# A two-block mixer kernel: first attention on split fp32r operands, modulation on TensorE in the recurrent stage, and values multiplied ahead of the turns

## Chip, cores and metric

The kernel runs on one core of a Trainium2 chip. The metric is the device time of one execution in microseconds, the median of the runs shown. TensorE is PE in the rows, its weight loads PEld, VectorE is DVE, ScalarE ACT, GpSimd POOL, and SP is the queue of SyncE, which issues most DMAs.

## What is computed

Two transformer blocks run one after the other on 512 tokens of width 1024, all in fp32. Each has a mixer and a mixture of experts. The change lies in the first mixer, in the modulation vectors of both blocks, and in the order of one shared loop:

```python
# modulation: one row per condition, six parts of 1024 columns
mod = silu(c) @ w_ada + b_ada                    # block 1
mod_2 = silu(c_2) @ w_mod_2 + b_mod_2            # block 2; parts 0 and 1 for c_ctx_2 too

# first mixer: u = layer_norm(x) * (1 + sc) + sh; proj = u @ w_in, split in q, k, v, f, xb, gb
cum = cumsum(log_sigmoid(f + b_f))               # 8 heads x 512 tokens
for i in range(4):                               # 128 queries each, keys up to their own tile
    logits = q_i @ k[:kend].T / 8 + cum_q - cum_k[:kend], causal mask
    out_i = softmax(logits) @ v[:kend]
# recurrent branch: conv over xb, gates r and ig by 64x64 blocks, h = a h + u, times gelu(gb)
mixed = concat(rms_norm(attn), rms_norm(lru)) @ w_out
```

The second block's mixer has two attentions of its own, a neighbourhood one with a bias and a grouped one, both of 8 heads and 4 query tiles, over 512 or 640 and over 768 keys.

## The kernel before

**Stages.** The program is a list of stages (`stage`, L64): each allocates its semaphores, gives every engine one instruction stream, and ends with a barrier of all engines (L70). So no engine goes on before the last one has run out, a queue of DMA issues included. In order: `setup`, `modulation` "mod1", `normalise` and `turn`, `project` "in1", `gates_and_lru`, `attention` "at1", `norm_branches` "nb1", `out_projection`, `normalise`, then the experts, then block two.

**Precision.** Products that need fp32 are made in two ways. `split3` (L45) takes operands split in a high and a low fp32r half and makes three products (L47 to L49); ACT rounds the high half and DVE subtracts to get the low one. Plain fp32 matmuls need no split; each shows in the trace as two instructions.

**Modulation.** Class `Modulation` (L285) makes one part of 1024 columns per job as a sum over 1024 rows of the weights: a quarter of a job, 256 rows or 1 MB, is loaded to a slot, and DVE adds it in two steps of 128 rows, each scaled by one silu column (L331, L335). Then TensorE sums the accumulator over the partitions by 8 products with a column of ones (`sum`, L353), DVE adds the bias (`put`, L365 to L371), and where a row is wanted in DRAM too, POOL stores it after all loads, element by element (`store`, L379), and waits for it to land. The steps are dealt out to turns of the stage beside which the jobs run, `per` of them to each (rounded up). Four jobs of block 1 run beside the ten chunks of "in1" (DVE makes the low half of chunk n+3 first, then its turn's steps; two slots, loaded from POOL's queue), eight jobs of block 2 beside the 32 units of "at1" (six slots, loaded from SP's queue).

**Input projection.** `project` (L548) streams ten chunks of w_in: SP loads, ACT makes the high half, DVE the low one, TensorE multiplies, ACT empties PSUM. TensorE takes the column sums of finished jobs two chunks later, and those of the last two chunks' turns at its end.

**Recurrent stage.** `gates_and_lru` (L690). POOL zeroes tiles (L711 to L713). SP loads the forget-gate weights (L718) and bias (L720), waits for the zeroing, loads 16 blocks of gate weights (L726), and then issues 64 small DRAM-to-DRAM copies of relative-position rows for block two (L732); nobody waits for those before block two. DVE runs the convolution (L743, L746) with the split of the forget weights in it (L753, L755), then the long chain of elementwise steps of both branches: softplus as a series (`log1p_series`), the cumulative sum `cum` (L780), the gates, the scan (L798) and the last product (L800). TensorE multiplies the forget logits (8 columns of weights, `split3`), then eight gate matmuls in plain fp32 (L814) into eight PSUM banks; ACT applies the sigmoids (L827).

**First attention.** `attention` (L842), 32 units of a head and a query tile. Per unit TensorE makes the scores in plain fp32 (L878: q by k with K = 64, minus `cum` by a selector with K = 8, the mask by the identity), DVE takes the maximum (L926), ACT the exponential (L962), DVE the inverse (L932) and the scaling (L935), TensorE turns the probabilities (L888), ACT copies them out of PSUM (L972), TensorE multiplies by the values (L898), DVE copies the result (L939). DVE's modulation steps lie between.

**Later attentions.** `attend` (L982) is the pipeline of block two. Same unit, but with operands split in fp32r halves: scores (L1051), turns (`fill`, L1037), ACT rounds the turned probabilities (L1095), DVE makes their low half (L1136), value products for two tiles at a time in two halves of a pair (`mix`, L1074 to L1076), ACT and DVE split the result (L1130, L1185). A turn waits for DVE's scaling (L1159) and for its PSUM bank; the first half of a pair waits for the low half of the pair's last tile (TensorE's loop, L1081):

```python
for u in range(STEPS):
    if u < NU:
        score(u)
    if 2 <= u <= NU + 1:
        turn_probs(u - 2)
    if mixing(u) is not None:
        mix(*mixing(u))
```

DVE's step u is: maximum of u (L1147), inverse and scaling of u-1, low half of u-2, then splits that hooks ask for.

## Time and profile before

| | |
|---|---|
| median of 3 runs | 3230.81 us (3228.14 to 3244.43) |
| profiled execution | 3230.41 us, of which the span 3228.7 us |
| mean granted TensorE clock over the span | 0.876 |
| busy, share of the span | PE 81%, PEld 66%, DVE 71%, ACT 48%, POOL 10% |
| HBM | 692.68 MB read, 227 GB/s over the span |
| "in1" | 69.5 to 199.5 us |
| recurrent stage | 199.5 to 267.7 us |
| first attention | 267.7 to 464.2 us |
| neighbourhood and grouped attention | 1394.4 to 1513.4 and 1513.4 to 1632.3 us |

### The profile page before, as it was taken

How to read it: one execution, taken by the hardware profiler on the slowest of the kernel's cores; microseconds unless marked ns; L12 is line 12 of the kernel's file. 1: busy time of each engine (PE TensorE's matmuls, PEld its weight loads, DVE VectorE, ACT ScalarE, POOL GpSimd, SP SyncE). 2: the span in 40 equal slices, each digit the busy share in tenths (PEclk: the TensorE clock that was granted, in tenths of full speed). 3: DMA queues.
4: the chain of work that ended last, by engine and by line, in shares of the span. 5: the costliest groups of instructions: out<-in, count | busy, mean ns of one | idle time of the engine just before them, and what ended most of it. 6: DMA issues, size and time to landing. Idle time of an engine off the chain costs nothing. (4 is left out here: it accounts for less than half of the span.)

```text
span 3228.7 us, 37865 instructions
## 1 busy us (share of the span) xinstructions
PE 2611.3 (81%) x12822; PEld 2126.6 (66%) x12822; DVE 2276.4 (71%) x2213; ACT 1539.0 (48%) x1420; POOL 316.6 (10%) x260
## 2 busy tenths in 40 slices
PE   2966975389996299857886379999999999999991
PEld 2844645367774199746766358778778778778771
DVE  5566645378885611277843579999999999999985
ACT  2212121066673323244622057666777666777660
POOL 0100000013331000000000011111111111111110
PEclk9985557589998599878998579999999999999995
DMA  5724421189995223100021189999999999999994
GB/s 203 240 46 149 123 73 52 61 328 379 377 371 217 95 67 110 57 1 27 1 86 59 40 293 362 363 370 367 367 366 362 364 368 369 367 366 362 364 343 150
DMA packets 256873, 731.66 MB, mean 227 GB/s; under 512 B 29779, under 2 KB 69906, under 8 KB 256594
## 3 DMA queue, kind: packets, MB, share of 16 engines
q1 hardware_dynamic: 232306, 653.93, 55.9%
q0 software_dynamic: 19872, 72.39, 5.8%
q10 hardware_dynamic: 4608, 4.20, 0.4%
q8 instruction: 52, 0.85, 0.1%
q14 instruction: 35, 0.29, 0.0%
HBM read 692.68 MB, written 39.37 MB: 227 GB/s over the span
## 5 line engine op out<-in xcount | busy, mean ns | idle before, releaser
L48 PE MATMUL psum_all<-sb_ring_r,sb_arena_r 128*128 128x512 f32 (+1 forms) x2912 | 1072.5, 368 | 1.2 <-issue 1.2
L152 DVE TENSOR_TENSOR sb_ring_r<-sb_ring,sb_hi_ring 128x2048 fp32r<-128x2048 f32 x297 | 674.4, 2287 | 277.3 <-ACT sb_hi_ring L143 271.6
L47 PE MATMUL psum_all<-sb_hi_ring,sb_arena_r 128*128 128x512 f32 (+1 forms) x1880 | 665.9, 354 | 51.6 <-DVE sb_ring_r L152 47.2
L49 PE MATMUL psum_all<-sb_hi_ring,sb_arena_r 128*128 128x512 f32 (+1 forms) x1880 | 660.0, 351 | 0.2 <-issue 0.2
L48 PEld LDWEIGHTS psum_all<-sb_ring_r,sb_arena_r 128*128 128x128 f32 x2912 | 558.0, 192 | 91.3
L143 ACT ACTIVATE sb_hi_ring<-sb_ring 128x2048 fp32r<-128x2048 f32 x297 | 563.4, 1913 | 103.0 <-DMA sb_ring<-in_w_gu_dram 30.6
L152 DVE TENSOR_TENSOR sb_ring_r<-sb_ring,sb_arena_r 128x2048 fp32r<-128x2048 f32 x258 | 581.4, 2283 | 23.5 <-ACT sb_arena_r L143 23.2
L143 ACT ACTIVATE sb_arena_r<-sb_ring 128x2048 fp32r<-128x2048 f32 x258 | 485.5, 1915 | 194.2 <-DMA sb_ring<-in_w_gu_dram 188.9
L47 PEld LDWEIGHTS psum_all<-sb_hi_ring,sb_arena_r 128*128 128x128 f32 x1880 | 360.4, 192 | 108.9 <-DVE sb_ring_r L152 49.4
L47 PE MATMUL psum_all<-sb_arena_r 128*128 128x512 f32 x1032 | 415.3, 402 | 12.6 <-DVE sb_ring_r L152 7.9
L49 PE MATMUL psum_all<-sb_arena_r 128*128 128x512 f32 x1032 | 412.0, 399 | 0.0
L49 PEld LDWEIGHTS psum_all<-sb_hi_ring,sb_arena_r 128*128 128x128 f32 x1880 | 359.5, 191 | 52.7 <-issue 1.3
L47 PEld LDWEIGHTS psum_all<-sb_arena_r 128*128 128x128 f32 x1032 | 195.3, 189 | 71.3 <-DVE sb_ring_r L152 28.9
L49 PEld LDWEIGHTS psum_all<-sb_arena_r 128*128 128x128 f32 x1032 | 196.1, 190 | 42.8
L1691 POOL DMA_INDIRECT y_dram<-sb_arena x52 | 95.1, 1829 | 997.8 <-ACT sb_arena L1842 988.9
L511 PE MATMUL psum_all<-sb_ident,sb_arena 128*128 128x128 f32 x176 | 40.2, 383 | 171.3 <-PEq L70 164.6
L511 PEld LDWEIGHTS psum_all<-sb_ident,sb_arena 128*128 128x128 f32 x176 | 27.7, 193 | 183.6 <-issue 166.2
L1677 POOL COPY sb_arena<-sb_ids 128x1 int32 (+1 forms) x54 | 24.5, 454 | 982.5 <-POOLq L70 467.4
L1817 ACT ACTIVATE sb_arena_r<-psum_all 128x1024 fp32r<-128x1024 f32 x54 | 55.1, 1020 | 115.0 <-PE psum_all L1720 96.8
L1892 DVE TENSOR_TENSOR sb_arena_r<-psum_all,sb_arena_r 128x1024 fp32r<-128x1024 f32 x54 | 65.6, 1215 | 62.0 <-ACT sb_arena_r L1817 62.0
L1837 ACT ACTIVATE sb_arena_r<-psum_all 128x1024 fp32r<-128x1024 f32 (+1 forms) x52 | 45.7, 878 | 116.6 <-PE psum_all L1729 116.6
L47 PE MATMUL psum_all<-sb_arena_r,sb_hi_ring 128*128 128x512 f32 (+1 forms) x224 | 86.9, 388 | 14.9 <-DVE sb_ring_r L152 14.9
(359 smaller groups left out, 3287.4 us busy)
## 6 DMA issues: line engine op xcount, KB each, us to landing
sb_ring<-in_w_gu_dram SPq DMA_DIRECT2D x272, 1024.0 KB, 7.1
sb_ring<-in_w_dn_dram SPq DMA_DIRECT2D x136, 1024.0 KB, 9.3
sb_ring<-in_w_e_gate_dram SPq DMA_DIRECT2D x36, 1024.0 KB, 7.3
sb_ring<-in_w_e_up_dram SPq DMA_DIRECT2D x36, 1024.0 KB
sb_ring<-in_w_e_down_dram SPq DMA_DIRECT2D x36, 1024.0 KB, 7.7
sb_ring<-in_w_in_dram SPq DMA_DIRECT2D x27, 1024.0 KB, 5.5
sb_ring<-in_w_mod_dram SPq DMA_DIRECT2D x24, 1024.0 KB, 5.8
sb_arena<-in_w_ada_dram POOLq DMA_DIRECT2D x16, 1024.0 KB, 5.6
```

The lines of the kernel that those rows point to most:

```text
L47: eng.matmul(out, a[0], b[0], start=start, stop=False)
L48: eng.matmul(out, a[0], b[1], start=False, stop=False)
L49: return eng.matmul(out, a[1], b[0], start=False, stop=stop)
L143: act.activation(s.hi[c % len(s.hi)], s.raw[c % SLOTS], ACT.Copy).then_inc(s.hi_made, 1)
L152: dve.tensor_tensor(s.lo[c % SLOTS], s.raw[c % SLOTS], s.hi[c % len(s.hi)].bitcast(F32), ALU.subtract).then_inc(s.lo_made, 1)
L511: ins = pe.transpose(k.psum[:, i % 2, t * P:(t + 1) * P], src[:, t, i * P:(i + 1) * P], k.ident[:])
L1677: pool.tensor_copy(idx, R.ids[:, bass.ds(j, 1)]).then_inc(s.idx, 1)
L1691: pool.indirect_dma_start(m.y, bass.IndirectOffsetOnAxis(ap=to_row.bitcast(U32), axis=0), ysb.rearrange("p h n -> p (h n)"), None).then_in ...
L1817: act.activation(part, banks, ACT.Copy).then_inc(s.x_hi, 1)
L1837: act.activation(part, banks, ACT.Copy).then_inc(s.h_hi, 1)
L1892: dve.tensor_tensor(part, banks, turned_banks(x_hi[p], KD)[0].bitcast(F32), ALU.subtract).then_inc(s.x_lo, 1)
```

## The change

The change moves the modulation, replaces the attention and swaps two calls.

- **Modulation.** Of the eight jobs that ran beside the attention two (parts 4 and 5 of block 2) now run beside "in1", which has six jobs. The other parts (0 to 3; 0 and 1 for both conditions) are multiplied on TensorE in the recurrent stage: 16 chunks of 1 MB (two groups of 2048 columns, 8 row blocks), four fp32 products of 512 columns each with a stationary operand of two silu columns, in PSUM banks 4 to 7. The gate matmuls share banks 0 to 3 and wait for ACT from the fifth on. Bias, gain and the stores follow in the next stage on POOL and SP; a turn in `norm_branches` brings the parts to columns.
- **Recurrent stage.** The forget logits are made three times, at rows 0, 32 and 64, so that `cum` can be split in three fp32r parts. SP's order: forget weights, zeroing, three bias loads, gate weights, the 16 chunks, then the 64 copies.
- **First attention.** `attention` is gone; `forgetting_attention` builds products for `attend`: scores of K = 128 on zero-padded fp32r halves, with `cum` by one fp32r product and the mask by another. The result isn't split.
- **`attend`**, for all three: TensorE multiplies the values ahead of the turns.

```diff
@@ gates_and_lru
+            pool.memset(w_parts.bitcast(F32), 0.0)
+            pool.memset(k.small[:, 100:101], 0.0)
             pool.memset(w_r, 0.0)
             pool.memset(w_i, 0.0).then_inc(s.zeroed, 1)
...
-            sp.dma_start(b_f, a["b_f"].rearrange("o h -> h o")).then_inc(s.f_loaded, 16)
             sp.wait_ge(s.zeroed, 1)
+            for group in range(3):
+                sp.dma_start(b_f[32 * group:32 * group + NH], a["b_f"].rearrange("o h -> h o")).then_inc(s.f_loaded, 16)
...
+            def load_mod(n):
+                c, kd = mod_chunks[n]
+                if n >= MOD_SLOTS:
+                    sp.wait_ge(s.mod_used, n - MOD_SLOTS + 1)
+                sp.dma_start(k.ring[:, n % MOD_SLOTS, :], a["w_mod_2"][0, kd * P:(kd + 1) * P, c * CHUNK:(c + 1) * CHUNK]
+                             ).then_inc(mod_landed[n % MOD_SLOTS], 16)
...
+            for n in range(len(mod_chunks)):
+                load_mod(n)
             rows = k.rpb_rows.rearrange("(r i) (h g c) -> h r i g c", i=16, h=NH, c=48)
...
-            dve.tensor_tensor_scan(cum, t1, z, 0.0, ALU.mult, ALU.add)
+            dve.tensor_tensor_scan(cum, t1, z, 0.0, ALU.mult, ALU.add).then_inc(s.summed, 1)
+            dve.wait_ge(s.part_hi, 1)
+            dve.tensor_tensor(t1, cum, fixed.parts[0:NF].bitcast(F32), ALU.subtract).then_inc(s.part_rest, 1)
...
+            def modulate(n):
+                c, kd = mod_chunks[n]
+                pe.wait_ge(mod_landed[n % MOD_SLOTS], 16 * (n // MOD_SLOTS + 1))
+                for b in range(CHUNK // 512):
+                    ins = pe.matmul(k.psum[32 * c:32 * c + 2, 4 + b, :], k.silu[:, KD + kd:KD + kd + KD + 1:KD],
+                                    k.ring[:, n % MOD_SLOTS, 512 * b:512 * b + 512], start=kd == 0, stop=kd == KD - 1)
+                ins.then_inc(s.mod_used, 1)
...
             ins.then_inc(s.multiplied, 1)
+            for n in range(4):
+                modulate(n)
             pe.wait_ge(s.loaded, 16 * 4 * NJ)
...
+                if i >= 4:
+                    pe.wait_ge(s.gated, i - 3)
+                pe.matmul(k.psum[:, i % 4, :], w[:, j, :], xc[:, j, :], start=True, stop=True).then_inc(s.gates, 1)
+            for n in range(4, len(mod_chunks)):
+                modulate(n)
...
+            act.wait_ge(s.mod_used, len(mod_chunks))
+            for c in range(2):
+                act.activation(mod_rows[32 * c:32 * c + 2], k.psum[32 * c:32 * c + 2, 4:8, :].rearrange("p b n -> p (b n)"),
+                               ACT.Copy).then_inc(s.mod_put, 1)
@@ attend
-                        pe.wait_ge(s.out_lo, h - 1)
+                        pe.wait_ge(s.out_hi, h - 1)
+                        if spec.splits:
+                            pe.wait_ge(s.out_lo, h - 1)
...
+                if mixing(u) is not None:
+                    mix(*mixing(u))
                 if 2 <= u <= NU + 1:
                     turn_probs(u - 2)
-                if mixing(u) is not None:
-                    mix(*mixing(u))
@@ forgetting_attention (new), products and values of one head
+        return [(cols, fixed.neg[:, h, :], fixed.parts[:, 0:n], True, False), (cols, q_hi, key_hi, False, False),
+                (cols, q_lo, key_hi, False, False), (cols, q_hi, key_lo, False, False),
+                (last, fixed.ident, fixed.causal, False, True)]
...
+        return [(v_hi[:, b, cols], v_lo[:, b, cols], b, int(b > 2 * pair), 2) for b in range(2 * pair + 2)]
...
+        def dve_step(dve, u, main):
+            if u < 2:
+                value_lo(dve, u)
+            if u % 8 == 4 and u < 24:
+                key_lo(dve, u // 8 + 1)
+            if u % TT == 1 and u < 28:
+                q_lo(dve, u // TT + 1)
@@ forgetting_attention, SP and POOL
+            sp.dma_start(bias_rows[0:2], b_mod[0:CHUNK].partition_broadcast(2)).then_inc(s.rows_loaded, 16)
...
+            sp.dma_start(k.mod_columns, mod_rows[0:2]).then_inc(s.rows_stored, 16)
...
+            pool.tensor_tensor(mod_rows[0:2], mod_rows[0:2], bias_rows[0:2], ALU.add).then_inc(s.row, 1)
@@ norm_branches
+            sp.dma_start(rows, columns[1]).then_inc(s.columns, 16)
...
+            pe.transpose(k.psum[:, 2, 0:4 * KD], rows, k.ident[0:4 * KD, 0:4 * KD]).then_inc(s.turned, 1)
@@ block_one_mixer
-             (w_1, 0, 5, 0, "plus one", mod["gt2"], None, gate[1:2, :])],
-             [(w_2, 1, 0, 1, "plain", mod["sh1_2"], None, None),
...
+             (w_1, 0, 5, 0, "plus one", mod["gt2"], None, gate[1:2, :]),
              (w_2, 1, 4, 1, "gain", mod["sc2_2"], g_ffn, gate[7:8, :]),
              (w_2, 1, 5, 1, "plain", mod["gt2_2"], None, gate[3:4, :])]]
```

In `setup` the selector `neg_sel` grows from 8 to 128 rows, by three selects in place of one (L243).

## Rows read from the trace of the kernel before

**Rows 1.** Five stages: us, busy of PE, PEld, DVE, ACT, POOL, clock, DMA, GB/s.

```profile
69.50:199.50 130.00, 123.04 (x640) 104.68 (x640) 61.66 (x46) 30.88 (x34) 15.25 (x20) 0.96 0.58 194
199.50:267.70 68.20, 16.12 (x40) 5.92 (x40) 56.59 (x81) 20.97 (x26) 1.03 (x3) 0.66 0.21 28
267.70:464.20 196.50, 185.64 (x560) 114.46 (x560) 115.50 (x203) 33.49 (x98) 3.53 (x4) 0.53 0.39 129
...
1394.40:1513.40 119.00, 89.21 (x624) 82.18 (x624) 98.31 (x199) 63.50 (x136) 1.89 (x2) 0.87 0.00 1
1513.40:1632.30 118.90, 95.69 (x652) 84.26 (x652) 96.03 (x182) 70.27 (x150) 0.00 (x0) 0.93 0.06 19
```

**Rows 2.** Groups by line, first attention: busy, mean ns | idle before.

```profile
L335 DVE SCALAR_TENSOR_TENSOR sb_arena<-sb_ring,sb_silu,sb_arena 128x1024 f32<-128x1024 f32 x56 | 70.5, 1279 | 1.7
...
L926 DVE TENSOR_REDUCE sb_small<-psum_all 128x1 f32<-128x128 f32 (+3 forms) x32 | 15.7, 490 | 36.8 <-PE psum_all L878 36.6
...
L935 DVE TENSOR_SCALAR sb_arena<-sb_arena,sb_small 128x128 f32<-128x128 f32 (+3 forms) x32 | 12.4, 387 | 1.2
...
L932 DVE RECIPROCAL sb_small<-sb_small 128x1 f32<-128x1 f32 x32 | 4.9, 154 | 0.6 <-DVE sb_arena L335 0.2
```

**Rows 3.** Timeline, input projection's end: start us, us, engine, line.

```profile
164.88 0.71 POOL L317 DMA_DIRECT2D sb_arena<-in_w_ada_dram  x1 [7.13 <-DVEq L339]
...
170.30 2.67 DVE L335 SCALAR_TENSOR_TENSOR sb_arena<-sb_arena,sb_silu 128x1024 f32<-128x1024 f32 x2 [2.88 <-DMA sb_arena<-in_w_ada_dram]
...
198.37 0.38 ACT L1311 ACTIVATE sb_arena<-psum_all 128x256 f32<-128x256 f32 x1 [2.45 <-PE psum_all L49]
```

**Rows 4.** Timeline at the end of the first attention.

```profile
449.50 3.57 PE L353 MATMUL psum_all<-sb_ones,sb_arena 128*128 128x1 f32 x16
...
464.17 0.99 SPq L122 DMA_DIRECT2D sb_ring<-in_w_out_dram  x2
```

**Rows 5.** Timeline of the recurrent stage.

```profile
200.06 0.52 POOL L713 MEMSET sb_rows<- 128x512 f32 x1
200.61 5.85 SPq L726 DMA_DIRECT2D sb_rows<-in_w_rg_dram  x8
...
211.91 41.11 SPq L732 DMA_DIRECT2D rpb_rows<-rpb_pad  x64
```

**Rows 6.** Timeline, the first attention's first weights.

```profile
267.69 3.37 SPq L317 DMA_DIRECT2D sb_ring<-in_w_mod_dram  x6
...
273.05 1.41 DVE L331 TENSOR_SCALAR sb_arena<-sb_ring,sb_silu 128x1024 f32<-128x1024 f32 x2 [2.78 <-DMA sb_ring<-in_w_mod_dram]
```

**Rows 7.** Weight loads of the gate matmuls at full clock.

```profile
218.08 0.19 PEld L814 LDWEIGHTS psum_all<-sb_arena,sb_rows 128*128 128x128 f32 x1 [0.24 <-issue]
218.51 0.19 PEld L814 LDWEIGHTS psum_all<-sb_arena,sb_rows 128*128 128x128 f32 x1 [0.24 <-issue]
```

**Rows 8.** The same table, short windows: eight-column products, gates, gates, attention.

```profile
206.90:210.40 3.50, 3.47 (x15) 1.19 (x13) 3.46 (x6) 0.00 (x0) 0.00 (x0) 0.98 0.11 23
213.30:217.00 3.70, 3.70 (x5) 1.58 (x6) 3.05 (x20) 2.23 (x3) 0.00 (x0) 0.57 0.27 38
217.00:220.70 3.70, 3.70 (x10) 1.60 (x9) 3.56 (x6) 2.59 (x5) 0.00 (x0) 0.97 0.24 37
272.00:292.00 20.00, 20.00 (x50) 10.38 (x49) 17.67 (x29) 4.51 (x14) 0.00 (x0) 0.50 0.92 369
```

**Rows 9.** A group by form, neighbourhood attention.

```profile
L1136 DVE TENSOR_TENSOR sb_hi_ring<-psum_all,sb_hi_ring 128x512 fp32r<-128x512 f32 x32 | 21.9, 685 | 2.9 <-ACT sb_hi_ring L1095 2.8
```

**Rows 10.** Timeline of a step of the grouped attention.

```profile
1561.30 0.85 PE L1037 MATMUL psum_all<-sb_ident,sb_rows 128*128 128x128 f32 x6
...
1562.02 0.87 ACT L1095 ACTIVATE sb_hi_ring<-psum_all 128x512 fp32r<-128x512 f32 x2 [1.02 <-PE psum_all L1037]
...
1562.99 1.02 DVE L1136 TENSOR_TENSOR sb_hi_ring<-psum_all,sb_hi_ring 128x512 fp32r<-128x512 f32 x2
...
1563.05 0.86 PE L1051 MATMUL psum_all<-sb_arena_r 128*128 128x512 f32 x4
```

More of the change, by code:

```diff
@@ L1022, in attend, with _ @@
         load_ahead(nc, k, block, name, ahead)
+        if hooks.sync is not None:
+            @block.sync
+            def _(sp):
+                hooks.sync(sp)
         def bank(m, n):
@@ L1180, in _ @@
                 hooks.dve_step(dve, u, s)
-                if leaving(u - 1) is not None:
+                if spec.splits and leaving(u - 1) is not None:
                     h = leaving(u - 1)
@@ L1185, in _, with norm_branches @@
                     dve.tensor_tensor(out_lo, k.psum[rows, 6 + h % 2, :], out_hi.bitcast(F32), ALU.subtract).then_inc(s.out_lo, 1)
-def norm_branches(nc, k, name, branches, squares, ahead=()):
+def norm_branches(nc, k, name, branches, squares, ahead=(), columns=None):
     NJ = DA // P
     with stage(nc) as ctx:
-        s = sems(nc, ctx, name, "squared", "summed", "chain", "mean", "root", "whole", "hi")
+        s = sems(nc, ctx, name, "squared", "summed", "chain", "mean", "root", "whole", "hi", "columns", "loaded", "turned")
+        rows = k.rows[0:4 * KD, 0, 0:P]
         block = ctx.enter_context(nc.Block())
-        load_ahead(nc, k, block, name, ahead)
+        @block.sync
+        def _(sp):
+            sp.dma_start(rows, columns[1]).then_inc(s.columns, 16)
+            for i, src in enumerate(ahead):
+                sp.dma_start(k.ring[:, i, :].rearrange("p (a b) -> p a b", a=src.shape[1]), src).then_inc(s.loaded, 16)
+            sp.wait_ge(s.loaded, 16 * len(ahead))
         @block.vector
@@ L1235, in _ @@
                                ACT.Copy).then_inc(s.hi, 1)
-def split_tiles(nc, k, name, tiles, ahead=()):
-    with stage(nc) as ctx:
-        s = sems(nc, ctx, name, "hi")
-        flat = lambda t: t.rearrange("p j n -> p (j n)")
-        block = ctx.enter_context(nc.Block())
-        load_ahead(nc, k, block, name, ahead)
-        @block.scalar
-        def _(act):
-            for whole, hi, _ in tiles:
-                act.activation(flat(hi), flat(whole), ACT.Copy).then_inc(s.hi, 1)
-        @block.vector
-        def _(dve):
-            for i, (whole, hi, lo) in enumerate(tiles):
-                dve.wait_ge(s.hi, i + 1)
-                dve.tensor_tensor(flat(lo), flat(whole), flat(hi).bitcast(F32), ALU.subtract)
+            act.wait_ge(s.turned, 1)
@@ L1346, in block_one_mixer @@
                   [area(4096, 4, T), area(6144, 4, T)],
-                  ahead=[column_chunk(a["w_out"][0], 256 * h) for h in range(AHEAD)])
+                  ahead=[column_chunk(a["w_out"][0], 256 * h) for h in range(AHEAD)],
+                  columns=(k.mod_turned, k.mod_columns.rearrange("c (j p) -> (c j) p", p=P)))
     out_projection(nc, k, "out1", a["w_out"][0], mixed, k.gate_rows[0:1, :], k.arena[:, 0:D])
@@ L2394, in grouped_attention @@
     spec.n = lambda t: KEYS
+    spec.splits = True
     spec.bias = None
```

317 lines of the change are left out of this document (153 added, 164 removed).

## The prediction

> **What bounds the kernel now.** I read the page first, then a table of the stages the diff touches, then their timelines, and the engines' groups last. The page's slices show the expert stages holding TensorE and DMA at nine tenths; nothing of the diff is there. In the stage table [rows 1] the first mixer's attention takes 196.5 us: TensorE is busy for 185.6 of it at a mean clock share of 0.53, so it works at the lower of its two levels (1.2 GHz). DVE is busy for 115.5, of which 71 are modulation sums [rows 2]. The recurrent stage before it takes 68.2 and has TensorE idle for 52; the input projection before that is TensorE's (123 of 130). The two later attentions take 119.0 and 118.9 with DVE busy for 98.3 and 96.0. Stages are closed by a barrier, so each is a sum of its own. The profiled execution took 3230.4, the median is 3230.8: the sum goes against 3230.4.
>
> **Part 1: input projection, two more modulation jobs.** Jobs go from 4 to 6, steps from 32 to 48, and so from 4 to 5 per chunk. A quarter of a job needs two DVE steps (2.67, 2.9 with what lies between) and comes into one of two slots: POOL issues at 164.88 and DVE begins at 170.30, so 5.4 to land [rows 3]. Two slots give one quarter per (5.4 + 2.9)/2 = 4.15. I placed the 48 steps turn by turn, five behind each low half: the last quarter is done at about 200.5. TensorE used to end just before 198.4 [rows 3]; a fifth job's column sum stands in its way, 3.57 at the low clock [rows 4], 1.9 at the full one, which makes it 200.2. So both end together, the sixth sum (1.9) comes behind, and behind it something new: its row is stored to DRAM as 1024 single elements. In the old attention the same tail ran from the sum's end at 453.07 to the next stage's first issue at 464.17: 11.1 [rows 4]. The next stage starts at 200.5 + 1.9 + 11.1 = 213.5 where it started at 199.5: **+14** (12, if the sums are full speed and nothing lags; 19, if the quarters lag by one landing).
>
> **Part 2: recurrent stage.** Its DVE chain moves by 4 to 6 us (memsets, three bias loads, six split instructions ahead; three part copies and two subtractions behind) and ends near +74: no longer the end. Two queues are.
> TensorE: POOL clears 1152 more columns, 1.2 by the 512 columns in 0.52 [rows 5], and SP's three bias loads now stand behind that, 1.4; the gate-weight loads took from 200.61 to 211.91, 11.3 [rows 5]. So the first 1 MB of modulation weights is issued at +15.1 and used 5.4 later, as in the old attention (267.69 to 273.05) [rows 6]: +20.5. Each chunk is four products of plain fp32 over 512 columns. The gate matmuls are such products: two instructions each, 0.43 apart at full clock [rows 7], so 0.86 a product and 3.43 a chunk. That the stationary side has 2 columns buys nothing: the forget logits with 8 columns stream like others. DMA delivers at 369 GB/s [rows 8], 2.8 us per MB, ahead of 3.43. After the wait the clock is low for 3.7 us as in 213.3 to 217.0 (0.57), then 0.97 [rows 8]: 1.9 lost. Four chunks end at +36.1, the gates at +43.0, the next eight at +70.4, the last four at +84; two PSUM reads of 2048 columns end near +88.
> SP: load 16 waits for chunk 12 of TensorE, +70.4. Behind it, on the same queue, stand the 64 relative-position copies, which ran under the DVE chain before: 41.1 in a row, 0.64 each, back to back [rows 5]. They end at +111.9. With 0.8 to the next stage (as 198.75 to 199.5) 112.7 against 68.2: **+44.5**. So moving the sums to TensorE is not what costs; what costs is the copies that are now queued behind its loads.
> What no row shows is how two stationary columns of fp32 hold the clock. Bounds: the full level (+44.5), as fp32 products of 128 columns had it and as products with 8 stationary columns had it (0.98) [rows 8]; or the low one throughout, as the old attention, with products of K = 8 and 64 in fp32, had it while TensorE never paused [rows 1]. Low costs (12 x 3.43 + 6.9 - 1.9) = 46 more. I take the full level, as K is 128 here and the rows are back to back.
> The Trainium skill (TensorE: Matmul & The Clock Gate, "Why this matters for your kernels") holds that a TensorE kept busy without a break has the full clock; by that there is only the first bound, but the old attention contradicts it: busy, and low.
>
> **Part 3: first attention.** The modulation sums (71 us of DVE and their first products) leave. What DVE now does: maxima 15.7, inverses 4.9, scaling 12.4 [rows 2]; the low halves of turned probabilities, new here, have the maxima's sizes and speed (0.685 at 512 columns) [rows 9]: 15.7, as the maxima; splits of queries, keys and values, 8 + 4 of 512 columns and 2 of 1024: 10.7. Together 59.4. The first later attention has the same pipeline and took 119.0 for 98.3 of DVE [rows 1]: as a factor (1.21) that gives 72, as an addition (20.7) 80. Part of either is waits that I count below, so I take 74. ACT, 63.5 there, is beside it here too. TensorE per head: 20 score products, 10 turns, 18 value products. Six turns take 0.60 and nine value products 1.15 [rows 10], so 0.12 apiece, and the wide scores 0.16 and 0.22: 6.3 a head, 50 in all. POOL's four row operations and SP's small loads and stores end within some 30 us and are hidden by the rest; no 9 us store is left at the end.
> The new order adds a wait. At an even step the value products need the low half of step u-3, DVE's last act of step u-1; the turns now queue behind them, and behind the turns ACT's rounding and DVE's next low half. Value products 0.54 + turns and their reading 0.54 + rounding 0.42 against maximum, inverse and scale 0.94: 0.6 late. Every other even step has a query split ahead that covers it, so 8 times: 4.5. **Stage 78 against 196.5: -118.5.** Bounds: 69 (half of the 20.7 and no wait), and 105 at the low clock: 48 instructions at 0.23 and 1.2 for the wide ones make 11.8 a head, 95, and 10 of filling.
>
> **Part 4: the two later attentions** change only in that order. In the grouped one DVE has no idle time in a normal step; turns start at 1561.30, ACT reads at 1562.02 (first copy done 1562.62) and DVE takes it at 1562.99 [rows 10]: 0.37 to spare. The new order puts 1.15 of value products (T to the next scores at 1563.05, less 0.60) ahead and starts them with DVE's last low half: about 1.0 late, on 8 even steps (the other 8 follow a late query fill that gives the time back): +8. In the neighbourhood one 0.45 x 8: +4. **+12**; from -3 (TensorE fills its wait for the scale, and scores come earlier) to +24 (all 16 even steps).
> Setup (two more POOL selects, 2 us, under the loads), the branch norm (one small load ahead of w_out, a turn and a copy at the end of idle engines): 0.
>
> **Sum.** 14 + 44.5 - 118.5 + 12 = -48: 3230.4 - 48 = 3182, at the median's level too.
>
> **Rivals.**
> R1, the clock stays low in both new places. For it: 0.53 over the old attention with TensorE always busy; the row says that work alone does not raise it. Against it: 0.97 on fp32 gates, 0.87 and 0.93 in the later attentions, which have the same fp32r operands and the same turns. Recurrent stage +46, attention +27: 3255, slower. Low clock in the recurrent stage alone already eats the gain, and anything above 48 us on top turns the sign.
> The Trainium skill (same page, "Part 4: PE-mode transpose") says that transposes do not engage the full clock; by that the attention with its 80 turns might stay low. The grouped attention with six per step has 0.93, so the trace disagrees.
> R2, low clock for the modulation products alone: 3228, no change.
> R3, attention low alone: 3209.
> R4, the order costs nothing and the attention fills at its lower bound: 3182 - 12 - 9 = 3161.
>
> **Chances.** Forecast 0.57 (3165 to 3205), R4 0.11, R3 0.06: faster 0.74. R2 0.15: same. R1 0.11: slower. Half a per cent, 16 us, is what a measurement here tells from no change. The range must leave out no more than 0.2: it reaches from below R4 (3152) to R2 (3231) and leaves out R1.
>
> **What would show it.** Recurrent stage near 113, TensorE idle for its last 28, SP in the 64 copies to its end; the projection's stage 14 longer with the last 9 to 11 waiting for POOL's store; attention near 78 with DVE the busiest and no sum in it; in the later attentions DVE idle ahead of low halves at every fourth step. Wrong, if products of modulation come 0.85 apart instead of 0.43 per instruction, or the copies cost less once weights are landing beside them, or the new attention is TensorE's.

## The result and the profile after

The changed kernel takes 3209.9 us (median of 6 runs, 3200.1 to 3213.1) against 3234.7 (6 runs) for the kernel before: ratio 0.9916, 95% interval 0.9892 to 0.9939, some 27 us faster. I had forecast 3182, 48 us faster, with a range of 3152 to 3231. The sign holds, the range holds the time, and the gain is about half of what I said.

The profiled execution took 3200.1 us, span 3198.4, the fastest of the six. In the same view as [rows 1], the five stages are now (us, busy of PE, PEld, DVE, ACT, POOL, clock, DMA, GB/s):

```profile
69.60:227.80 158.20, 128.87 (x672) 110.22 (x672) 81.27 (x65) 30.89 (x34) 22.71 (x30) 0.91 0.65 213
227.80:337.60 109.80, 69.91 (x168) 17.86 (x168) 60.52 (x87) 27.94 (x33) 4.83 (x8) 0.81 0.56 170
337.60:421.50 83.90, 60.25 (x384) 54.87 (x384) 61.75 (x142) 44.98 (x119) 16.02 (x4) 0.83 0.01 2
1345.70:1474.00 128.30, 90.56 (x624) 85.06 (x624) 98.25 (x199) 63.28 (x136) 1.83 (x2) 0.86 0.00 1
1474.00:1602.80 128.80, 95.44 (x652) 85.31 (x652) 96.49 (x182) 68.71 (x150) 0.00 (x0) 0.92 0.05 17
```

Against [rows 1] that gives a ledger, each stage being closed by a barrier:

| stage | before | after | measured | forecast |
|---|---|---|---|---|
| input projection | 130.0 | 158.2 | +28.2 | +14 |
| recurrent stage | 68.2 | 109.8 | +41.6 | +44.5 |
| first attention | 196.5 | 83.9 | -112.6 | -118.5 |
| neighbourhood attention | 119.0 | 128.3 | +9.3 | +4 |
| grouped attention | 118.9 | 128.8 | +9.9 | +8 |
| sum | | | -23.6 | -48 |

The sum of the five agrees with the difference of the medians (24.8) and with the ratio. The profiled execution shows 30.3 because some stages that the change doesn't touch were 7 us shorter in it; the stretch from the first load of block one's output projection to the load for its last normalisation, experts included, takes between 590 and 605 us over the eleven profiles of this case that send the same tokens to the same experts, with nothing changed in it. So below I go by stages, and by totals only where runs were repeated.

**Input projection.** Timeline of the end of the stage (start us, us, engine, line, and the idle time before it):

```profile
199.50 2.67 DVE L336 SCALAR_TENSOR_TENSOR sb_rows<-sb_arena,sb_silu,sb_rows 128x1024 f32<-128x1024 f32 x2 [3.11 <-DMA sb_arena<-in_w_mod_dram]
202.22 3.57 PE L354 MATMUL psum_all<-sb_ones,sb_rows 128*128 128x1 f32 x16 [2.45 <-DVE sb_rows L336]
205.83 0.17 DVE L366 TENSOR_TENSOR sb_mods<-psum_all,sb_bias_cols 128x8 f32<-128x8 f32 x1 [3.15 <-PE psum_all L354]
206.29 0.88 POOL L380 DMA_DIRECT2D gate_rows<-sb_mods  x1 [2.43 <-DVE sb_mods L366]
227.89 0.11 POOL L720 MEMSET sb_arena<- 128x12 f32 x1 [20.72 <-POOLq L70]
```

The last quarter is added by 202.2 (I had 200.5), the last store is issued at 206.3, and from that issue to the next stage it is 21.5 us in which no engine works. The reading of the store's line in this kernel, and of the same line before, tells why:

```profile
L380 POOL DMA_DIRECT2D gate_rows<-sb_mods x6: 883/884/916, 194.6 to 206.3; - x6
DMA to landing us min/median/max: 13.5/16.4/18.8
```
```profile
L379 POOL DMA_DIRECT2D gate_rows<-sb_mods x8: 883/883/923, 168.5 to 453.6; - x8
DMA to landing us min/median/max: 8.5/9.2/10.3
```

Before, a row of 1024 single elements landed 9.2 us after its issue. Now all six are issued between 194.6 and 206.3, since POOL stores only after all its loads, and the last of these goes out at 193.9. They land 13.5 to 18.8 after their issues: at 208.1, 211.4, 212.3, 216.0, 219.8 and 224.4, so 3.3 apart in the mean. What they do in that time the DMA records don't show. The stage table has the DMA share at 0.11 from 202 to 210, at 0.02 to 214, and then

```profile
214.00:218.00 4.00, 0.00 (x0) 0.00 (x0) 0.00 (x0) 0.00 (x0) 0.00 (x0) 0.50 0.00 0
```

and so on to 226: three of the six land while no DMA engine has a packet on record.

**Recurrent stage.** Timeline of TensorE, then of ACT, then of SP:

```profile
246.59 15.34 PE L844 MATMUL psum_all<-sb_ring,sb_silu 128*2 128x512 f32 x32 [4.06 <-DMA sb_ring<-in_w_mod_dram]
268.93 39.65 PE L844 MATMUL psum_all<-sb_ring,sb_silu 128*2 128x512 f32 x96
308.62 3.76 ACT L900 ACTIVATE sb_arena<-psum_all 2x2048 f32<-2x2048 f32 x2 [16.37 <-PE psum_all L844]
295.25 41.11 SPq L760 DMA_DIRECT2D rpb_rows<-rpb_pad  x64
337.61 0.27 SPq L1219 DMA_DIRECT2D sb_arena<-in_b_mod_dram  x1
```

The modulation products come 0.41 apart (39.65 / 96), and the stage table over 32 us of them has the clock at 1.00:

```profile
273.00:305.00 32.00, 32.00 (x80) 6.32 (x79) 21.20 (x14) 13.28 (x15) 0.00 (x0) 1.00 0.82 273
```

So fp32 products with two stationary columns held the full level here, and R1 and R2 are out. TensorE and ACT are done at 312.4; SP is in its 64 copies from 295.25 to 336.4, and the next stage begins at 337.6. The copies start at +67.4 where I had +70.4.

**First attention.** DVE is the busiest (61.8 us; I had 59.4), and no sum is left in it. The clock is 0.50 up to 362, with TensorE busy for half of that time, and 0.97 from there on. The start looks unlike the rest. Its timeline, POOL and DVE:

```profile
340.00 4.53 POOL L1232 TENSOR_TENSOR sb_arena<-sb_arena 1x2048 f32<-1x2048 f32 x1 [107.13 <-DMA sb_arena<-in_b_mod_dram]
342.76 2.85 DVE L1261 TENSOR_TENSOR sb_ring_r<-sb_arena,sb_ring_r 128x1024 fp32r<-128x1024 f32 x1 [1.47 <-ACT sb_ring_r L1257]
344.59 5.37 POOL L1233 TENSOR_TENSOR sb_arena<-sb_arena 2x2048 f32<-2x2048 f32 x1
345.53 0.41 DVE L1075 TENSOR_REDUCE sb_small<-psum_all 128x1 f32<-128x256 f32 x1
346.05 4.00 DVE L1087 TENSOR_SCALAR sb_rows<-sb_rows,sb_small 128x128 f32<-128x128 f32 x1
```

A scaling of 128 columns takes 4.00 us where the same one takes 0.29 later; the maximum from PSUM between them is not long. A value split takes 2.85, the next one 1.21. Both lie beside POOL's row operations: the scaling ends with POOL's second one (350.05 and 349.96), and the split ends 1.1 behind the end of the first (345.61 and 344.53), which is about what a split takes alone.

**Later attentions.** Two neighbouring steps of the grouped attention, the pipeline that [rows 10] show before:

```profile
1524.40 0.38 PE L1002 MATMUL psum_all<-sb_hi_ring,sb_arena_r 128*128 128x256 f32 x1 [0.83 <-DVE sb_hi_ring L1064]
1525.56 0.82 PE L963 MATMUL psum_all<-sb_ident,sb_rows 128*128 128x128 f32 x6
1526.26 0.88 ACT L1023 ACTIVATE sb_hi_ring<-psum_all 128x512 fp32r<-128x512 f32 x2 [1.81 <-PE psum_all L963]
1526.89 1.02 DVE L1064 TENSOR_TENSOR sb_hi_ring<-psum_all,sb_hi_ring 128x512 fp32r<-128x512 f32 x2 [0.95 <-ACT sb_hi_ring L1023]
```

Value products wait for a low half, turns stand behind them, then ACT, and DVE comes to its next low half 0.95 us before that is ready. That is the chain I had drawn, and its size (1.0). How often it happens stands in the reading of the low halves' line, idle time in us and times, first the neighbourhood and then the grouped attention:

```profile
  ACT sb_hi_ring L1023: 14.7, 10
...
  ACT sb_hi_ring L1023: 10.6, 10
```

Before, the same two were 2.8 us in 2 times and 1.6 us in 2 times.

### The profile page after: what moved, and what is told of

The parts are those of the page before. It is cut to its first block and busy times, and to the rows that moved or that the text cites. A ratio compares the mean times of both kernels' runs of the same rounds, so it can differ in the third digit from the quotient of the medians.

```text
span 3198.4 us, 37782 instructions
## 1 busy us (share of the span) xinstructions
PE 2542.9 (80%) x12807; PEld 2082.1 (65%) x12807; DVE 2246.0 (70%) x2177; ACT 1555.4 (49%) x1451; POOL 326.8 (10%) x277
## 5 line engine op out<-in xcount | busy, mean ns | idle before, releaser
L1707 POOL COPY sb_arena<-sb_ids 128x1 int32 (+1 forms) x54 | 26.4, 488 | 1053.9 <-POOLq L70 485.9
L47 PE MATMUL psum_all<-sb_arena_r,sb_hi_ring 128*128 128x512 f32 (+2 forms) x232 | 91.3, 394 | 43.7 <-DVE sb_hi_ring L786 28.8
L1023 ACT ACTIVATE sb_hi_ring<-psum_all 128x512 fp32r<-128x512 f32 (+3 forms) x144 | 63.9, 478 | 112.0 <-PE psum_all L963 111.1
```

The costliest lines, as they stand in the source:

```text
L47: eng.matmul(out, a[0], b[0], start=start, stop=False)
L1023: act.activation(dst, src, ACT.Copy).then_inc(s.rounded, 1)
L1707: pool.tensor_copy(idx, R.ids[:, bass.ds(j, 1)]).then_inc(s.idx, 1)
```

## The experiments

Totals are given against the kernel before on the same chip, stages from the profile. Stages that an edit doesn't touch stayed where they were, unless said.

### Turns first again, and values first alone

```diff
@@ attend, TensorE
-                if mixing(u) is not None:
-                    mix(*mixing(u))
                 if 2 <= u <= NU + 1:
                     turn_probs(u - 2)
+                if mixing(u) is not None:
+                    mix(*mixing(u))
```

> The changed kernel with one thing undone: in all three attentions the turns stand ahead of the value products again. My theory (the order makes DVE's next low half late at nearly every even step) expects the neighbourhood attention back from 128.4 to about 119 us, the grouped one from 128.9 to about 119, and the first attention from 84.0 to 79 or 80: some 24 us in all, 3210 to 3186. The rival (the 19 us in the two later attentions come from something else, such as the clock or the data's place after the change) expects them to stay at 128 and 129. A second rival, for the first attention alone: it was written for the new order and loses by the old one; then it takes more than 84.

Measured: 3180.1, ratio 0.983 (0.9803 to 0.9858), 30 us less than the changed kernel's 3209.9.

```profile
338.20:414.00 75.80, 58.23 (x384) 52.56 (x384) 61.00 (x142) 45.76 (x119) 16.02 (x4) 0.85 0.01 2
1351.10:1469.10 118.00, 87.51 (x624) 80.36 (x624) 98.33 (x199) 63.46 (x136) 1.82 (x2) 0.89 0.00 1
1469.10:1587.90 118.80, 95.68 (x652) 84.30 (x652) 95.94 (x182) 70.28 (x150) 0.00 (x0) 0.93 0.05 19
```

All three stages give back what the order took: 8.1, 10.3 and 10.0. The same line of low halves is now

```profile
  ACT sb_hi_ring L1023: 2.0, 2
...
  ACT sb_hi_ring L1023: 1.6, 2
```

much as before the change. The first attention, written for the new order, is faster in the old one too, by 8.1 where I had counted 4.5.

The mirror of it is the kernel before with only these two calls swapped (in the two later attentions, as the first has its own loop there):

> The kernel before with one part of the change alone: in the two later attentions the values are multiplied ahead of the turns. The changed kernel lost 9.3 and 10.0 us in these two stages, and undoing the order there gave 10.4 and 10.0 back. If the order is all of it, the two stages take 129 and 129 here as well, instead of 119.0 and 118.9, and the kernel 3234 + 20 = 3254. The rival (half of the loss comes with other parts of the change) expects 3244 or less.

Measured: 3257.7, ratio 1.0062 (1.0041 to 1.0083), 20 us slower by the ratio; the two stages take 128.5 and 129.2. The order is all of the loss in the later attentions, and it needs nothing else of the change.

### Copies between the weight loads

```diff
@@ gates_and_lru, SP
             rows = k.rpb_rows.rearrange("(r i) (h g c) -> h r i g c", i=16, h=NH, c=48)
-            for h in range(NH):
-                for turned_row in range(GRID_H):
+            copies = [(h, turned_row) for h in range(NH) for turned_row in range(GRID_H)]
+            for n in range(len(mod_chunks)):
+                load_mod(n)
+                for h, turned_row in copies[4 * n:4 * n + 4]:
```

> The changed kernel with SP's 64 relative-position copies dealt out, four behind each of the 16 weight loads of the recurrent stage, instead of all 64 behind the last load. My theory (the stage ends when SP's queue has issued them) expects TensorE's last modulation product at +81 as now, two PSUM reads of ACT behind it, and the stage at 85 to 86 us instead of 109.4: 24 less, 3210 to 3186. The rival (the copies are cheap, and what holds the stage is TensorE or DMA) expects no more than 5 us. A third way: the copies between the loads make the weights late, since four take 2.6 us and a chunk 3.3, and TensorE ends later than +85; then a part of the 24 comes back.

Measured: 3185.7, ratio 0.9856 (0.9837 to 0.9875), 24 us less. The stage's row in the stage table:

```profile
225.50:312.80 87.30, 70.28 (x168) 17.70 (x168) 60.53 (x87) 27.93 (x33) 4.82 (x8) 0.91 0.62 214
```

and ACT's timeline at its end:

```profile
308.23 3.76 ACT L900 ACTIVATE sb_arena<-psum_all 2x2048 f32<-2x2048 f32 x2 [18.32 <-PE psum_all L844]
312.87 0.63 ACT L1242 ACTIVATE sb_ring_r<-sb_arena 64x512 fp32r<-64x512 f32 x1 [0.89 <-PEq L70]
```

109.8 becomes 87.3: the copies' queue was the end, now TensorE and ACT's two reads are. The third way that I had allowed for shows a little: two of the first four chunks are waited for, 0.67 and 1.01 us, the modulation products behind the gates start at +43.0 instead of +41.1, and the stage is 1.3 longer than the 86 I had at most.

### A quarter of the products

```diff
@@ gates_and_lru
-        mod_chunks = [(c, kd) for c in range(2) for kd in range(KD)]
+        mod_chunks = [(c, kd) for c in range(2) for kd in range(2)]
```

> The changed kernel with 4 of the 16 chunks of modulation in the recurrent stage (rows 0 to 255 of the weights; the other three quarters of each sum are left out), all before the gates; the 64 copies stay behind the loads. If the stage ends when SP's queue has issued the copies, and these start when the last load is out, then the copies run from +18 to +59, TensorE is done at +45, and the end is DVE's chain, which ended at +73.7 in the changed kernel: the stage takes 75 to 77 instead of 109.4. That is also what the twelve chunks behind the gates and the copies behind them cost together: 33. The rival (DVE's own chain is stretched by products and landing weights beside it) expects less than 72.

Measured: the stage takes 75.1 us. Its last DVE instruction in the timeline:

```profile
298.19 2.29 DVE L835 SCALAR_TENSOR_TENSOR sb_arena<-sb_arena 128x2048 f32<-128x2048 f32 x1
```

DVE's chain ends at +74.3 and sets the end, as I had placed it at +74. So the stage has three ends: DVE's chain at 75, TensorE and ACT at 85 to 87, SP's copies at 109. Its total (3210.5) is of no use, since other modulation sends other tokens to the experts.

### The rows' landing awaited later

```diff
@@ project, POOL
                 mod.load(pool)
-                mod.store(pool)
+                mod.store(pool, k.gates_stored)
@@ forgetting_attention, SP
             sp.wait_ge(s.rows_stored, 48)
+            sp.wait_ge(k.gates_stored, 96)
```

With the semaphore given, `store` increments that one and doesn't wait.

> The changed kernel with POOL's six row stores issued as now beside the input projection, but their landing awaited by SP at the end of the first attention instead of by POOL at the end of the stage. By my reading (158.2 us of which the last 21 are nothing but this wait) the stage ends right behind POOL's last issue at 207.2, so 138 instead of 158.2: 20 less, 3210 to 3190, and nothing given back later. The rival (six stores of 1024 single elements still load the DMA engines, and the next stage's weight loads stand behind them) expects the recurrent stage to grow by up to 15, and the gain to be 5 to 10.

Measured: 3209.5, ratio 0.992 (0.9893 to 0.9947): nothing won, and neither theory had that. Nobody waits for the rows in the stage any more, and yet POOL's timeline shows:

```profile
208.05 0.88 POOL L380 DMA_DIRECT2D gate_rows<-sb_mods  x1 [1.50 <-DVE sb_mods L366]
227.05 0.11 POOL L720 MEMSET sb_arena<- 128x12 f32 x1 [18.12 <-POOLq L70]
```

The stage takes 157.9. POOL stands at the barrier for 18.1 us with its last instruction an issue, and all other engines have run out. The last of the six was the slowest, 16.9 from its issue, so it landed at 225.0 and the barrier passed at 227.05. So here the stage did not end before POOL's own stores had landed, without any wait for them in the program. This is one run; whether the barrier waits for the landing or for something in POOL that ends about then, no run separates.

### The rows from SP

```diff
@@ project
                 mod.load(pool)
-                mod.store(pool)
@@ project, SP, behind its loads
+            if mod is not None:
+                mod.store(sp)
```

> The changed kernel with the six row stores issued by SP, which has nothing left to do from 124 us on, as soon as each job's columns are there, instead of by POOL behind all its weight loads. If the tail of 21.5 us behind the last issue is six stores in series on one queue, four of them issued only from 194.6 on since POOL's loads come first, then here four are long landed, and the last one needs what a single store needed before the change, 9 to 11: the stage ends near 217 instead of 227.8, 11 less, 3199. The rival (one such store takes 21 by itself, whenever it is issued) expects 158 as now.

Measured: 3227.0, ratio 0.998 (0.9964 to 0.9995), 17 us slower than the changed kernel. The stage takes 176.9, against both theories. Its row in the stage table:

```profile
69.50:246.40 176.90, 133.28 (x672) 113.88 (x672) 81.21 (x65) 30.89 (x34) 17.54 (x24) 0.85 0.62 191
```

and one of POOL's loads in the timeline:

```profile
207.08 0.75 POOL L318 DMA_DIRECT2D sb_arena<-in_w_mod_dram  x1 [12.50 <-DVEq L340]
```

Five of the stores land in 9.3 to 11.7 us, as a single one did before; the sixth, issued 2.4 us behind the fifth, takes 16.9. So one is as quick from SP as from POOL, and two close together stand in line (they land at 236.3 and 245.5). What costs is new: POOL's weight loads, whose issues waited 2.2 to 6.2 us for DVE from 108 us on in the changed kernel, now wait 12.3 and 12.5 in the stretch with stores under way (issued at 172.7 and 189.3), and the last one goes out at 215.5 instead of 193.9.

### The rows in the next stage

```diff
@@ project, POOL
-                mod.store(pool)
@@ gates_and_lru, POOL, behind its memsets
+            for row, name in ((0, "gt1"), (4, "sh2"), (5, "sc2"), (1, "gt2"), (7, "sc2_2"), (3, "gt2_2")):
+                pool.dma_start(k.gate_rows[row:row + 1, :].rearrange("o (k p) -> p (o k)", p=P), k.mod[name],
+                               allow_slow_non_contiguous=True).then_inc(s.row_stored, 16)
+            pool.wait_ge(s.row_stored, 96)
```

> The changed kernel with the six row stores moved from the input projection to POOL's stream in the recurrent stage, behind its memsets. The run with the late wait showed that a stage does not end before POOL's own stores have landed, whoever waits for them; so they must leave the stage, and POOL is idle for a hundred us in the next one. Expected: the input projection ends at DVE's last bias sum, 137 to 138 us instead of 158.2; the recurrent stage stays within 2 of 109.4; in all 20 less, 3210 to 3190. The rival (the stores' single elements stand in the way of the gate weights and of the first modulation chunks, as the stores from SP's queue did with the weights in the projection) expects the recurrent stage longer by 10 to 20, and little or nothing won.

Measured: 3208.9, ratio 0.9925 (0.9903 to 0.9948): nothing won, the rival's case and worse. The projection drops from 158.2 to 134.4, the recurrent stage grows from 109.8 to 134.8. The stage table, with 30 us of the latter by themselves:

```profile
69.50:203.90 134.40, 126.52 (x672) 108.22 (x672) 81.37 (x65) 30.68 (x34) 17.47 (x24) 0.96 0.74 251
203.90:338.70 134.80, 70.55 (x168) 18.09 (x168) 61.20 (x87) 27.82 (x33) 10.08 (x14) 0.75 0.74 139
213.00:243.00 30.00, 6.60 (x21) 3.54 (x19) 26.54 (x51) 3.97 (x5) 1.16 (x2) 0.61 1.27 23
```

and TensorE's first modulation products in the timeline:

```profile
247.39 3.58 PE L847 MATMUL psum_all<-sb_ring,sb_silu 128*2 128x512 f32 x4 [27.80 <-DMA sb_ring<-in_w_mod_dram]
```

The third line is the point: from 213 to 243, with the stores issued from 208.9 on, the DMA records overlap (so their share is over 1) and 23 GB/s are moved. The DMA view of the same 30 us says whose records these are (packets, MB, share):

```profile
q1 hardware_dynamic: 886, 0.68, 122.4%
q0 software_dynamic: 125, 0.02, 3.5%
```

The first queue is SP's, with the weights, the second POOL's, with the stores. So it is not the stores' own packets that fill the time: SP's packets are under way for long beside them. The first modulation chunk is issued at 217.5 and used at 247.4, 30 us instead of 5.1, as TensorE waits 27.8 for it. The stage grows by 25.0, so, as an estimate from that, a row of 1024 single elements holds up what shares the DMA engines with it by some 4 us. In the projection the rows had nothing behind them to hold up but the barrier.

The Trainium skill (DMA: Bandwidth & Descriptors, "Why small descriptors are slow (HBM only)") says that each descriptor carries a fixed cost besides its bytes. By that it is the 6144 elements that are paid for and not the 24 KB, and the run with the turned rows below agrees. Where the time goes is open: with the stores on SP's queue that queue shows 6240 packets in 3.0% of the engines' 108 us, which is 8 ns apiece, far less than the delay.

### Three edits together

Turns first, copies between, rows in the next stage.

> The changed kernel with three edits together: turns ahead of value products again, the 64 copies between the weight loads, and the row stores in the recurrent stage. If the three costs are independent, as the stages with barriers between them say: 3210 - 28 (turns first, by its runs) - 23 (copies between, by its runs) - 20 (row stores out of the tail) = 3139, 0.970 of the kernel before. The rival is that the row stores and the copies share DMA in the recurrent stage, and its end moves from 87 to 95 or more: then 3145 to 3155.

Measured: 3154.7, ratio 0.9756 (0.9724 to 0.9787). The rival's case: the recurrent stage takes 110.2 where the copies between alone gave 87.3, so the rows cost 23 here too. The other two edits add up: by themselves they took 29.8 and 24.2 off 3209.9, which leaves 3155.9.

### Rows turned on TensorE

```diff
@@ gates_and_lru
+            pe.transpose(k.psum[0:48, 1, 0:P], k.mod_late, k.ident[:]).then_inc(s.row_turned, 1)
...
+            act.wait_ge(s.row_turned, 1)
+            act.activation(k.rows[0:48, 1, 512:512 + P], k.psum[0:48, 1, 0:P], ACT.Copy).then_inc(s.row_read, 1)
...
+                if n == 5:
+                    sp.wait_ge(s.row_read, 1)
+                    for i, row in enumerate((0, 4, 5, 1, 7, 3)):
+                        sp.dma_start(k.gate_rows[row, :].rearrange("(k p) -> k p", p=P),
+                                     k.rows[KD * i:KD * i + KD, 1, 512:512 + P]).then_inc(s.row_stored, 16)
```

In place of POOL's six element stores, on top of the other two edits; `mod_late` are the 48 columns of the six jobs.

> The kernel of the three edits, but with the six gate rows made in another way: one turn on TensorE brings the six sets of eight columns to 48 rows of 128, ACT copies them out, and SP stores them in six transfers of eight packets of 512 bytes, where POOL stored 6144 single elements. My theory, formed now from the run that moved the stores to the recurrent stage (134.8 us there instead of 109.4, with the gate weights and first modulation chunks landing at 10 to 60 GB/s over 25 us), is that single elements keep the DMA engines busy for some 4 us a row, wherever they are put. Then the recurrent stage takes 87 to 89 instead of 110.2, the input projection stays at 134, and the kernel takes 3155 - 22 = 3133. The rival (it is the place, ahead of the gate weights, that costs, or TensorE and ACT pay for the turn) expects 100 or more for the recurrent stage.

Measured: 3130.2, ratio 0.9689 (0.9669 to 0.9709). The two stages in the stage table:

```profile
69.50:203.70 134.20, 126.31 (x672) 108.08 (x672) 81.30 (x65) 30.88 (x34) 17.44 (x25) 0.96 0.74 251
203.70:291.00 87.30, 70.58 (x169) 17.50 (x169) 60.42 (x87) 28.09 (x34) 4.82 (x8) 0.91 0.63 214
```

and the stores in SP's timeline:

```profile
235.28 2.01 SPq L759 DMA_DIRECT2D gate_rows<-sb_rows  x6
```

The projection keeps its 134, the recurrent stage its 87.3. The same 24 KB in 48 packets of 512 bytes cost 2.0 us of SP's queue, which had them to spare. This edit changes three things together, the form of the transfers, their queue and their moment. That the queue is not it follows from the run with single elements on SP's queue, where the weights were late too; single elements at this later moment were not tried.

### No row operations on POOL

```diff
@@ forgetting_attention, POOL (two memsets of one element each stand in their place)
-            pool.tensor_tensor(mod_rows[32:33], mod_rows[32:33], bias_rows[32:33], ALU.add)
-            pool.tensor_tensor(mod_rows[0:2], mod_rows[0:2], bias_rows[0:2], ALU.add).then_inc(s.row, 1)
-            pool.tensor_scalar(gained, gained, 1.0, None, ALU.add).then_inc(s.row, 1)
-            pool.tensor_tensor(gained, gained, bias_rows[0:2, D:2 * D], ALU.mult).then_inc(s.rows_made, 1)
```

> The changed kernel without POOL's four operations on the modulation rows in the first attention (two bias sums over 2048 columns, plus one, times gain: the two mods parts of block two they serve are left without bias and gain; two memsets of one element stand in their place). In the changed kernel they ran from 340.0 to 356.3, and five DVE instructions in that time are long: a scaling of 128 columns 4.00 us (0.29 later), two value splits 2.85 and 1.21, a query split 1.41 (0.68), a scaling of 384 columns 1.60 (0.42). My theory, formed now, is that POOL's row operations hold DVE up: without them the excess of some 7.5 us goes, and the attention takes 76 to 78 instead of 84.0. The rival (DVE was long for another reason, such as waits inside the instruction for ACT) expects 83 to 84.

Measured: the attention takes 76.6 instead of 83.9 (its total isn't comparable, for the reason given above). The instructions that were long are now, in DVE's timeline,

```profile
342.43 1.23 DVE L1257 TENSOR_TENSOR sb_ring_r<-sb_arena,sb_ring_r 128x1024 fp32r<-128x1024 f32 x1 [1.47 <-ACT sb_ring_r L1253]
344.09 0.29 DVE L1087 TENSOR_SCALAR sb_rows<-sb_rows,sb_small 128x128 f32<-128x128 f32 x1
```

1.23 for 2.85 and 0.29 for 4.00. DVE's busy time falls from 61.8 to 54.5, by 7.2, which is the stage's gain. POOL's four operations held DVE up while it was the busiest engine of the stage.

The Trainium skill (SBUF — State Buffer, "🔬 SBUF: two separate sides") describes one pair of SBUF ports that VectorE and GpSimd share by an exclusive lock held for a whole instruction; VectorE needs it for two SBUF inputs, beside a GpSimd operation that reads SBUF, or in a mode that uses two ports. By that the split of two SBUF tiles should wait, the scaling in SBUF too if it runs in such a mode (which no view here shows), and the maximum read from PSUM should not: the trace agrees (2.85 and 4.00 against 0.41, where it is 0.42 without POOL).

### Bias and gain on DVE

```diff
@@ gates_and_lru, DVE, at its end (ACT's two reads and POOL's four operations leave)
+            dve.wait_ge(s.bias_loaded, 48)
+            for c, rows in enumerate((slice(0, 2), slice(32, 33))):
+                dve.wait_ge(s.mod_used, KD * (c + 1))
+                dve.tensor_tensor(mod_rows[rows], k.psum[rows, 4:8, :].rearrange("p b n -> p (b n)"), bias_rows[rows],
+                                  ALU.add).then_inc(s.mod_put, 1)
+                if c == 0:
+                    dve.wait_ge(s.mod_put, 1)
+                    gained = mod_rows[0:2, D:2 * D]
+                    dve.scalar_tensor_tensor(out=gained, in0=gained, scalar=1.0, in1=gain_rows, op0=ALU.add, op1=ALU.mult)
```

> The same, and the bias and gain of the modulation rows made by three DVE operations that read PSUM at the end of the recurrent stage, in place of ACT's two reads there and of POOL's four operations in the first attention. Without POOL's four the attention took 76.6 instead of 84.0; with turns first it took 75.9, so both together should give 69 or 70. The recurrent stage has DVE done at +74 and TensorE at +81: one sum over 2048 columns (some 2.3 us by DVE's rate elsewhere) stands behind TensorE in place of ACT's two reads, so 85 to 88. In all 6 to 8 less than the kernel with the turned rows: 3126. Rival: DVE's sums read PSUM at half the speed or wait for the gains that SP loads last, and the recurrent stage gives 4 or more back.

Measured: 3125.7 (5 runs, 3119.5 to 3126.4), ratio 0.9663 (0.9646 to 0.968), 109 us less than the kernel before by the ratio, against the 27 of the changed one. Recurrent stage and attention in the stage table:

```profile
206.40:291.30 84.90, 71.65 (x169) 17.97 (x169) 66.30 (x90) 24.36 (x32) 4.82 (x8) 0.90 0.65 221
291.30:361.40 70.10, 57.04 (x384) 51.75 (x384) 53.81 (x142) 45.67 (x119) 0.00 (x0) 0.91 0.01 1
```

and DVE's last sum in the timeline:

```profile
288.42 2.28 DVE L853 TENSOR_TENSOR sb_arena<-psum_all,sb_arena 1x2048 f32<-1x2048 f32 x1 [0.36 <-PE psum_all L866]
```

The recurrent stage is just below the 85 to 88 expected, the attention as expected. The total is 4.5 below the kernel with the turned rows where the two stages say 8.9; in this profile the projection took 2.7 more (136.9), and the two medians' spreads (3119.5 to 3126.4, and 3126.5 to 3136.1) don't settle the rest.

## Why the prediction was right or wrong

**Part 1 failed, and is the largest error: +28.2 for +14.** The steps and the quarters were placed well (202.2 for 200.5). The fifth column sum was not in the way at the end, as I had it: it ran from 185.0 to 186.9. The sixth took 3.57 at the low clock where I had 1.9. These two make 3.4 of the error. The other 10.9 is the step "the same tail ran from the sum's end at 453.07 to the next stage's first issue at 464.17: 11.1": here it is 22.0, from 205.8 to 227.8. That tail was of one row that was alone in its queue. Here POOL holds back all six until its last load is out, and they land one behind another, the last 18.1 after its issue. I had read where the stores stand in POOL's stream and did not count how many come together. A hint was there, 9.2 to land for a row of 4 KB where 1 MB lands in 5.4, but no row of the kernel before shows such stores landing in series.

**Part 2 was right: +41.6 for +44.5**, and for the reasons given. Copies' start at +67.4 (forecast +70.4), DVE's end at +73.7 (+74), the full clock under the products (0.41 apart), 41.11 for the copies. Dealing the copies out shows that they cost 22.5 of it, and the run with a quarter of the products that DVE's chain alone would allow 75. The 3 us that it came out less are the first products, at +18.8 for +20.5 (the loads go out at +13.7 for +15.1), and the eight chunks behind the gates, which at 0.41 an instruction took 26.4 for 27.4.

**Part 3: -112.6 for -118.5**, the right mechanism with three terms off. "POOL's four row operations ... are hidden by the rest" failed: they cost 7.3 (76.6 without them), by making DVE's own instructions long and not by being waited for. The order's wait was 8.1 and not 4.5. And the base of 74 was 4 too high: with neither it is 70.1, just under the factor's 72 and far from the addition's 80. The two costs overlap: each was taken out with the other in place, and together they are 13.8 (83.9 to 70.1) and not 15.4. Why the later attention has more idle time than this one was not tried.

**Part 4: +19.2 for +12**, the mechanism shown twice (by the order undone, and by the order alone). In the grouped attention 0.95 late for 1.0, but 10 times and not 8. In the neighbourhood one "0.45 x 8" failed: the low halves wait 14.7 us in 10 places. Its TensorE is at the low level in some of them: from 1410.0 to 1413.4 the clock is 0.51, a value product of 256 columns takes 0.41 (0.28 at the full level), ACT waits 3.93 for the turns behind the products, and DVE waits 2.27 for its low half at 1414.35.

The sum of the errors is 14.2 - 2.9 + 5.9 + 7.2 = 24.4, and the largest single piece of it, 10.9, lies in a tail in which no engine works. The time, 3209.9, lies outside the 3165 to 3205 to which I had given 0.57. That the range holds it is luck in part: it reached so far up for R2, whose condition did not come, and not for any of the errors above. Rivals: R1 and R2 are excluded by the clock over the products (1.00). In the attention it was low for the first 24 us and then 0.97, so R3, low throughout, is excluded too; that the time fell near R3's 3209 is no merit of R3. R4's first half (the order costs nothing) is excluded by both runs on it.

## What to carry to other kernels

Before a store goes in front of a barrier, count its packets and how many such stores come together: a row of 1024 single elements held up what shared the DMA engines with it by some 4 us here (25 us for six), and moving them to another queue, a later wait or another stage only moved the cost. Make the row contiguous first (one turn and a copy). When an engine is the bound, ask not only what it waits for but what makes its own instructions longer: compare the duration of the same form with and without another engine beside it. And what a queue issues in order is a term of its own, to be placed like an engine's work: 64 copies that nobody in the stage needs ended it, and dealt out between waits they cost 1.9 us at most.

## What the runs showed of the hardware

- In one run a stage with POOL stores under way did not end before they had landed, though nothing in the program waited for them (18.1 us at the barrier, which passed at 227.05, the last landing being at 225.0).
- Beside six stores of 1024 single elements the weights on the other queue moved at 23 GB/s over 30 us, with packets of that queue on record at 122% and of the stores' queue at 3.5%; the same bytes in 48 packets of 512, from SP, left the stage at 87.3 us.
- The last three of six such stores landed while the DMA engines had no packet on record (share 0.00 from 214 to 226 us).
- POOL's operations on one or two partitions of 2048 columns made DVE's instructions on SBUF operands up to 4.00 us long (0.29 without them), and left one that reads PSUM as it was (0.41).
- Plain fp32 products with two stationary columns ran at the full clock, 0.41 us per instruction of 512 columns.
